# Weights of gates, branches, output and queries laid out by blocks in HBM

## The reference, cut to what matters

```
u    = einsum('btcw,cwd->btcd', stack([o_a, o_b, o_m]), W['w_branch'])   # 3 branches, 512 -> 1024
gate = sigmoid(xn @ W['w_gate']).reshape(b, t, 3, 1024)                  # 1024 -> 3072
h    = x + sum(gate * u, axis=2) @ W['w_out']                            # 1024 -> 1024
f    = peer(rmsnorm(h, W['ln_ffn']))                                     # below
y    = h + f

peer: q = xb @ W['w_pq']                       # 1024 -> 1024, queries of 8 heads x 2 halves
      scores against sub_keys, top 16 of each half, top 16 of the 256 sums -> 16 experts per head
      a = gelu(einsum(u_tab[e], xb));  out = einsum(softmax(top) * a, v_tab[e])
```

## Time and profile before

| | us |
|---|---|
| median of 3 runs | 2643.17 |
| lowest, highest | 2639.89, 2653.09 |
| span of the profiled execution | 2647.1 |
| PE, DVE busy | 1829.5 (69%), 1743.8 (66%) |
| ACT, POOL busy | 681.6 (26%), 865.0 (33%) |

### The profile page before, as it was taken

How to read it: one execution, slowest core, us unless ns; L and a number is a source line. 1 busy time by engine, 2 the same in 40 slices (tenths; PEclk the granted TensorE clock), 3 DMA queues, 4 the chain that set the end, 5 groups by cost and what they waited for, 6 DMA issues and landing times.

```text
span 2647.1 us, 25199 instructions
## 1 busy us (share of the span) xinstructions
PE 1829.5 (69%) x6665; PEld 996.3 (38%) x6665; DVE 1743.8 (66%) x3900; ACT 681.6 (26%) x2066; POOL 865.0 (33%) x829
## 2 busy tenths in 40 slices
PE   7999889699855756882558757677675443884355
PEld 3467466454322212331232217454453322561021
DVE  3453465631147796665889998888646886786685
ACT  2010166430112332332223322222222221231122
POOL 1000033210005543332345445322343777332242
PEclk9999889799978887996779985688897565557676
DMA  4121240034309889998999789999988999989997
GB/s 147 36 93 64 60 153 2 1 120 151 135 17 371 345 360 373 371 359 323 400 407 391 315 334 380 349 331 333 347 326 313 343 381 400 390 339 381 365 373 318
DMA packets 200776, 727.63 MB, mean 275 GB/s; under 512 B 39769, under 2 KB 83186, under 8 KB 133754
## 3 DMA queue, kind: packets, MB, share of 16 engines
q0 software_dynamic: 84384, 577.16, 54.6%
q1 hardware_dynamic: 114386, 144.15, 16.0%
q10 hardware_dynamic: 1864, 4.71, 0.5%
HBM read 717.36 MB, written 12.66 MB: 276 GB/s over the span
## 4 chain that ended last, share of the span: by engine, by line
DMA 17%; PE 14%; DVE 13%; issue 11%; SPq 9%; POOL 4%; ACT 1%; DVEq 0%; ACTq 0%; POOLq 0%
SPq L1322 4%; SPq L1321 4%; DMA fq_wb<-in_w_branch 4%; DVE heads_t L3344 3%; DMA branch_rows_t<-in_uv_tab,e_idx 3%; PE fq_mg_g_ps L2974 2%; DMA ex_pairs<-in_uv_tab,e_idx 2%; DMA heads_t<-in_uv_tab,e_idx 2%; PE ex_y_ps L3411 2%; PE sl_at_l_ps L1986 1%; DMA cmp_k_t<-in_uv_tab,e_idx 1%; PE fq_mg_ps L2969 1%; DVE ex_pairs L3349 1%; POOL branch_rows_t L3317 1%; DMA is_ch<-in_cache_a_kidx,chunk_rows 1%
## 5 line engine op out<-in xcount | busy, mean ns | idle before, releaser
L3377 ACT ACTIVATE ex_coef<-ex_dots 128x1 f32<-128x1 f32 x512 | 103.7, 203 | 1014.7 <-DVE ex_dots L3349 968.4
L3317 POOL DMA_INDIRECT ex_pairs<-in_uv_tab,e_idx x147 | 185.3, 1260 | 531.4 <-issue 273.3
L3317 POOL DMA_INDIRECT branch_rows_t<-in_uv_tab,e_idx x163 | 194.0, 1190 | 294.3 <-DVE heads_t L3344 164.6
L3317 POOL DMA_INDIRECT heads_t<-in_uv_tab,e_idx x146 | 184.9, 1267 | 296.1 <-DVE heads_t L3344 166.7
L3349 DVE CUSTOM_DVE_ANT_0 branch_rows_t<-branch_rows_t,heads_t 128x1024 f32<-128x1024 f32 x163 | 198.9, 1221 | 49.9 <-DMA branch_rows_t<-in_uv_tab,e_idx 48.5
L3349 DVE CUSTOM_DVE_ANT_0 ex_pairs<-ex_pairs,heads_t 128x1024 f32<-128x1024 f32 x147 | 179.6, 1222 | 64.4 <-DMA ex_pairs<-in_uv_tab,e_idx 63.0
L825 PE MATMUL in_acc<-in_w,xn_t 128*128 128x512 f32 (+7 forms) x560 | 209.2, 530 | 5.5 <-POOLq L184 3.8
L3349 DVE CUSTOM_DVE_ANT_0 heads_t<-heads_t 128x1024 f32<-128x1024 f32 x146 | 178.3, 1222 | 49.5 <-DMA heads_t<-in_uv_tab,e_idx 48.4
L1347 PE MATMUL cs_pp<-cs_ch,xn_t 128*128 128x256 f32 x512 | 130.2, 419 | 59.4 <-DMA cs_ch<-in_cache_cmp_kv 59.4
L3344 DVE SCALAR_TENSOR_TENSOR heads_t<-branch_rows_t,ex_coef,heads_t 128x1024 f32<-128x1024 f32 x112 | 143.6, 1282 | 32.8 <-issue 21.4
L3411 PE MATMUL ex_y_ps<-ex_pairs,heads_t 128*128 128x512 f32 x208 | 108.9, 652 | 77.2 <-ACT heads_t L3384 70.5
(11 more groups left out here) (740 smaller groups left out, 3456.2 us busy)
## 6 DMA issues: line engine op xcount, KB each, us to landing
cs_ch<-in_cache_cmp_kv SPq DMA_DIRECT2D x256, 128.0 KB, 6.6
fq_wg<-in_w_gate SPq DMA_DIRECT2D x6, 2048.0 KB, 25.2
in_w<-in_w_in SPq DMA_DIRECT2D x4, 2048.0 KB, 11.5
first_w<-in_w_gate SPq DMA_DIRECT2D x3, 2048.0 KB, 8.1
fp_wb<-in_w_branch SPq DMA_DIRECT2D x6, 1024.0 KB, 10.3
fp_wg<-in_w_gate SPq DMA_DIRECT2D x3, 2048.0 KB, 8.1
fq_wb<-in_w_branch SPq DMA_DIRECT2D x6, 1024.0 KB, 32.3
fs_blocks<-in_w_branch SPq DMA_DIRECT2D x6, 1024.0 KB, 26.9
```

The source lines that it names most:

```text
L3317: pool.indirect_dma_start(out=pair(s), out_offset=None, in_=i["uv_tab"], in_offset=bass.IndirectOffsetOnAxis(ap=idx[:, t, m:m + 1], axis=0 ...
L3377: act.activation(c, dots[:, t, m:m + 1], ACT.Gelu_apprx_tanh).then_inc(gelu_done, 1)
```

## The change

The host lays the four weights out anew before the launch: `w_gate` as 6 blocks and `w_branch` as 6 blocks, numbered 2c+q, `w_out` and `w_pq` as 2 blocks each. In a block, partition p's part is one contiguous run, 16 KB (8 KB for `w_branch`), in the order in which it lies in SBUF. The kernel reads block n as `[p][k][512]`. Number, size, order, queue and semaphores of the DMAs stay as they are, and so do the tiles in SBUF and every instruction of the other engines.

```diff
+    def block_of(self, name, n):
+        return self.i[name][n].rearrange("p (k n) -> p k n", n=512)
...
-                    sp.dma_start(self.first_w[:], self.i["w_gate"][:, :512].rearrange("(k p) n -> p k n", p=P)).then_inc(self.first_w_in, 16)
+                    sp.dma_start(self.first_w[:], self.block_of("w_gate", 0)).then_inc(self.first_w_in, 16)
...
-                after = [(2, out_w[0][0], i["w_out"][:, :512].rearrange("(k p) n -> p k n", p=P), out_w[1][0]),
+                after = [(2, out_w[0][0], self.block_of("w_out", 0), out_w[1][0]),
...
                 def half(name, b):
-                    return i[name][:, 512 * b:512 * b + 512].rearrange("(k p) n -> p k n", p=P)
+                    return self.block_of(name, b)
...
-                            sp.dma_start(wg[j % depth], i["w_gate"][:, D * c + 512 * q:D * c + 512 * q + 512].rearrange("(k p) n -> p k n", p=P)).then_inc(w_in[j % depth], 16)
-                        sp.dma_start(wb[:, j % depth], i["w_branch"][c, :, 512 * q:512 * q + 512].rearrange("(k p) n -> p k n", p=P)).then_inc(w_in[j % depth], 16)
+                            sp.dma_start(wg[j % depth], self.block_of("w_gate", 2 * c + q)).then_inc(w_in[j % depth], 16)
+                        sp.dma_start(wb[:, j % depth], self.block_of("w_branch", 2 * c + q)).then_inc(w_in[j % depth], 16)
...
-                        sp.dma_start(wb[:, j], i["w_branch"][c, :, 512 * q:512 * q + 512].rearrange("(k p) n -> p k n", p=P)).then_inc(w_in[j], 16)
+                        sp.dma_start(wb[:, j], self.block_of("w_branch", 2 * c + q)).then_inc(w_in[j], 16)
...
+        if name == "w_gate":
+            a = a.reshape(KD, P, 3, 2, 512).transpose(2, 3, 1, 0, 4)
+            a = _np.ascontiguousarray(a).reshape(6, P, KD * 512)
+        if name == "w_branch":
+            a = a.reshape(3, 4, P, 2, 512).transpose(0, 3, 2, 1, 4)
+            a = _np.ascontiguousarray(a).reshape(6, P, 4 * 512)
+        if name in ("w_out", "w_pq"):
+            a = _np.ascontiguousarray(a.reshape(KD, P, 2, 512).transpose(2, 1, 0, 3)).reshape(2, P, KD * 512)
```

More of the change, by code:

```diff
@@ L2770, in finish_rows @@
                 pq_w = ([pairs[2], pairs[0]], [self.gather_sem(f"{tag}_pq_in{b}") for b in range(2)])
-                after = [(2, out_w[0][0], i["w_out"][:, :512].rearrange("(k p) n -> p k n", p=P), out_w[1][0]),
-                         (4, out_w[0][1], i["w_out"][:, 512:].rearrange("(k p) n -> p k n", p=P), out_w[1][1]),
-                         (6, pq_w[0][0], i["w_pq"][:, :512].rearrange("(k p) n -> p k n", p=P), pq_w[1][0])]
-                then = [(1, pq_w[0][1], i["w_pq"][:, 512:].rearrange("(k p) n -> p k n", p=P), pq_w[1][1])]
+                after = [(2, out_w[0][0], self.block_of("w_out", 0), out_w[1][0]),
+                         (4, out_w[0][1], self.block_of("w_out", 1), out_w[1][1]),
+                         (6, pq_w[0][0], self.block_of("w_pq", 0), pq_w[1][0])]
+                then = [(1, pq_w[0][1], self.block_of("w_pq", 1), pq_w[1][1])]
             if not last:
```

## The result

The changed kernel takes a median of 2614.7 us (2613.91 to 2615.88, 4 runs) against 2646.09 us (2639.89 to 2653.09, 4 runs) beside it: a ratio of 0.9864, interval 0.9828 to 0.9900. Run once more beside the later experiments it gave 2611.15 us against 2645.11, ratio 0.9881 (0.9859 to 0.9902). The profiled execution has a span of 2612.9 us against 2647.1, at a granted clock of PE of 0.806 against 0.805. The forecast was 2607 us, 36 less than before; it is 31.4 less between these medians and 34.2 less between the spans.

A forecast was written before the change was run, and what follows sets the result against it. Two limits were assumed: weights that come late and the DMA's total. The terms -26 - 2 - 8 = -36 us took the span from 2647.1 to 2611.1; from 2643.2 the forecast was 2607 us, range 2588 to 2641.

The forecast's parts named there:

- Turns by packets, and 16 KB runs as 16 KB packets: DMA queues: an engine takes one packet from each queue in turn; 16 KB runs become 16 KB packets of 626 ns.
- A job's load of 12.5 + 2.8 us: Weight loads beside gathers: 7.5 us for the gate block, 5.0 us for the branch block, about 2.8 us until landing.
- `fq` merge, -26: `fq` merge: first load lands earlier, two later waits of 9 us go, less store and gather delays: -26 us.
- The 4 us that were added for late gathers: `fq` merge: gathers are late next, beside weights and the `w_out` block; 4 us allowed, giving 1196 us.
- `fq` after the merge, -2: Rest of `fq`, 1225 to 1385 us: one 2 MB block and `ln_ffn` come sooner; -2 us, between 0 and -8.
- the first wait alone, -15: Start of the `fq` merge: the least gain, if only PE's first wait for weights shrinks, -15 us.
- `fs`, -8: `fs`: waits for `ln_ffn` and branch blocks shrink by up to 12 us each, bytes stay; -8 us, between 0 and -12.
- Issues are as many as before: DMA issues: their number stays and no wait is added; no term in the sum.
- The rest: Outside `fq` and `fs`: `fp` is PE's, 0 to -0.5 us; the tail 0, between -4 and +4 us.
- The bound of a turn near 4 KB: Rival, DMA queues: a turn is bounded near 4 KB, weights get a third of the bandwidth; 2620 us, chance 0.12.
- The gathers set the pace: Rival: gathers lose what weights gain, DVE stands for gathers; only packet efficiency left, 5.9 us, 2637 us, chance 0.12.
- The slower rival: Rival, `fq` and `fs`: weight bursts hold up gathers, 5.2 us of DVE stall per 2 MB block; 2667 us, chance 0.08.

The follow-up runs named there:

- e6: Only the loads of jobs 0 and 1 of the `fq` merge come by blocks, other loads row by row as in the kernel before: 2640.57 us, ratio 0.9989 to it.

## Why the prediction was right, step by step

*Turns by packets, and 16 KB runs as 16 KB packets*: both right, by the count of packets, by the four sizes and by the order of the packets. A 16 KB packet takes 612 to 625 ns in the stretch shown, 626 forecast.

*A job's load of 12.5 + 2.8 us*: PE starts 15.1 us after the first issue of `fq` (990.67 to 1005.76), 15.3 forecast for the landing. The median of the six is 16.7 us.

*`fq` merge, -26*: PE's end moved by -34.6 us from the stage's start (forecast -34.2) and the two later waits, of 9.00 and 7.97 us, went. With them went the slow products behind them: a job's first 16 matmuls take 8.35 and 8.34 us after these waits and 7.03 without one (the clock granted from 1084 to 1093 us of before was 0.84). The store was put at +4.4; the chain shows +5.8 (18.15 against 12.37), and DVE's return moved by -29.0. The 4 us that were added for late gathers are thus 3 too many: PE waited for no gather-driven stall of DVE in the merge. DMA was full, as the sum of the bytes from the other side had it.

*`fq` after the merge, -2*: +0.3. It was held to gain from weights that come sooner. But from DVE's return to the end of the stage DVE is busy 149.6 of 163.8 us before and 148.9 of 164.2 after, at a DMA share of 0.97 and 0.96: DVE's work sets most of the length there, and that did not change. The forecast for the whole of `fq`, -28, met -28.7 with two errors that cancel; that is luck.

*The least, "the first wait alone, -15"*: too large. e6 shows 7.6 us in the stage for it and less than 0.3% in the kernel.

*`fs`, -8*: -7.9, though not in the way it was worked out. `ln_ffn` waits 4.07 us, not 14.96, and lands 5.78 us after its issue (6 to 8 forecast). Of the 10.9 us that this wait lost, the stage got little: behind the six branch blocks it is 3.3 us shorter (106.4 for 109.7), and the 45 us behind the wait stayed 45, where 4.5 were hoped for. But the chain's piece for the branch blocks grew from 21.66 to 26.84 us instead of shrinking: it now ends with a later block. PE's first product comes after 9.1 us (2366.33 to 2375.4), not 10.4 (2391.31 to 2401.7); to the transposes behind the six blocks it is 39.2 us, not 43.8, and these 4.6 us are the larger part of the 7.9.

*"Issues are as many as before"*: true of their number, but not of what they cost SP, which the prediction left out of its sum. It is the last section's subject.

*The rest*: -1.3 in the tail, within its -4 to +4; its two lengths, some 6 us apart, go with PE's clock. The 0.0 in the middle is chance, as said above.

*The rivals.* The bound of a turn near 4 KB is refuted by the share of 0.72; its time, 2620, was mispriced besides, since a kernel with that share takes 2612.58. It had counted 10 us for the first wait and 3 for `fs`: the first wait is 5 to 6 us longer, and fq is 3.0 and fs 3.1 us longer than in the changed kernel's first profile. "The gathers set the pace" was half right: DVE does wait more for gathers (the page of the profile gives 187.0 us of waiting before the dots on `ex_pairs`, `branch_rows_t` and `heads_t`, 159.9 before the change), but PE's jobs no longer wait, and the idle 8% of the DMA in the merge is used up. The slower rival would have shown DVE's stalls of 5 us per block passed on to PE. The stalls are there: from PE's first product to its last in the merge DVE waits 38.4 us for gathers, up to 5.64 at a time (7.4 us and 1.4 before). But they stand ahead of 15 of 50 dots, and PE's jobs still follow at 27.76 us. That the seven buffers refill between the bursts fits this and was not tested.

## What to carry to other kernels

Where two DMA queues compete, count packets, not bytes: the queue with short runs gets the small share, and laying its data out in longer runs moves that share without moving a byte more. Most of the gain is there once the transfer lies under the work that waits for it (here from 2 KB to 4 KB); beyond that, with the DMA engines full, 8 KB gave 6 us more in the two stages and nothing that the kernel's time could show, and 16 KB no more. Then look at what small transfer stands behind the large ones in the same queue: issuing a store ahead of 4.2 MB of weights, where it had taken 18 us to land behind them, gave about 8 us more. And before a difference of a few microseconds between two profiles is put down to an edit, look at PE's clock in that stretch and at a second profile of the same kernel.

## What was not expected of the hardware

With 2 KB runs SP itself was held up while it issued. SP's timeline, first of the kernel before, then of the changed one, at the start of `fq` and of `fs` (start, duration of the issue or of several merged):

```profile
989.77 23.04 SPq L2941 DMA_DIRECT2D fq_wb<-in_w_branch  x1
...
2391.31 24.64 SPq L3032 DMA_DIRECT2D fs_blocks<-in_w_branch  x6
```

```profile
991.99 0.47 SPq L2945 DMA_DIRECT2D fq_wb<-in_w_branch  x1
...
2366.33 2.91 SPq L3036 DMA_DIRECT2D fs_blocks<-in_w_branch  x6
```

In the kernel before, the fourth load of `fq` held SP for 23.04 us and the six branch blocks of `fs` for 24.64 us, one of them 13.25 us; with 4 KB runs the longest of the six took 4.40 us and with 16 KB 0.61. Three loads (2560 packets of 2 KB) had been issued within 2.8 us ahead of the long one. That SP waited for room in its queue is the likely reading, not shown. So the size of a run also decides when SP reaches its next instruction: `x_sample`, next in SP's order, was issued 24.7 us into `fs` before (2415.99) and 3.0 us into it now (2369.28). How much of the 4.6 us that `fs` gained in its first part is owed to this, and how much to the share, was not separated. In `fq` the first wait is owed to the share: the two loads that PE waited for were issued at 987.00 and 987.41, ahead of the hold.
